# Residual additions of a feed-forward chunk placed between the next tile's taps, and squares summed later at its end

## The reference, cut to what matters

```
def conv_ffn(h, w_up, w_conv, b_conv, w_down):
    a = h @ w_up                                   # 1024 -> 5632
    a = conv1d(a, w_conv, width 3, causal, per channel) + b_conv
    g, val = split(a, 2)
    return (silu(g) * val) @ w_down                # 2816 -> 1024

x = x + conv_ffn(rms_norm(x, norm_ffn_g), w_up, w_conv, b_conv, w_down)
x = rms_norm(x, norm_final_g)                      # end of the first block
hx = modulate(rms_norm_2(x, norm_g), shift, scale) # start of the second block
p = hx @ a_w_in                                    # q, k, v and gate of the second block
```

## Time and profile before

| what | value |
|---|---|
| median of 3 runs | 3227.45 us (3226.65 to 3232.88) |
| the profiled execution | 3229.67 us, its span 3228.0 us, 44121 instructions |
| TensorE busy, matmuls | 2946.4 us, 91% |
| VectorE busy | 1726.4 us, 53% |
| GpSimd busy | 1067.0 us, 33% |
| ScalarE busy | 981.2 us, 30% |
| mean granted TensorE clock | 0.961 |

### The profile page before, as it was taken

How to read it: one execution, slowest core, us unless ns; L and a number is a source line. 1 busy time by engine, 2 the same in 40 slices (tenths; PEclk the granted TensorE clock), 3 DMA queues, 4 the chain that set the end, 5 groups by cost and what they waited for, 6 DMA issues and landing times. The chain is left out here.

```text
span 3228.0 us, 44121 instructions
## 1 busy us (share of the span) xinstructions
PE 2946.4 (91%) x16440; PEld 2420.9 (75%) x16440; DVE 1726.4 (53%) x2485; ACT 981.2 (30%) x1727; POOL 1067.0 (33%) x657
## 2 busy tenths in 40 slices
PE   3789899999999999989999997888889698999998
PEld 2578787777777777768877887878878477867776
DVE  4654254574455554555557337878752553067753
ACT  1112164321111111141101206767740200167731
POOL 1433312554554444432223221322233432311222
PEclk6899999999999999999999999999999899999999
DMA  2354460121111111113335312121111032342111
GB/s 85 126 171 157 126 137 21 33 72 39 45 47 57 46 39 44 40 39 114 126 129 182 131 60 106 51 98 50 58 35 39 24 123 93 111 119 53 28 40 66
DMA packets 214038, 255.18 MB, mean 79 GB/s; under 512 B 9385, under 2 KB 182766, under 8 KB 213886
## 3 DMA queue, kind: packets, MB, share of 16 engines
q1 hardware_dynamic: 198306, 189.68, 19.7%
q10 hardware_dynamic: 15584, 63.51, 5.0%
HBM read 187.56 MB, written 65.60 MB: 78 GB/s over the span
## 5 line engine op out<-in xcount | busy, mean ns | idle before, releaser
L977 PE MATMUL ps<-hh,w_parts 128*128 128x512 f32 (+2 forms) x2560 | 1000.7, 391 | 75.8 <-POOL hl L797 34.7
L978 PE MATMUL ps<-hl,w_parts 128*128 128x512 f32 (+2 forms) x2560 | 983.9, 384 | 0.0
L979 PE MATMUL ps<-hh,w_parts 128*128 128x512 f32 (+2 forms) x2560 | 981.3, 383 | 0.0
L977 PEld LDWEIGHTS ps<-hh,w_parts 128*128 128x128 f32 x2560 | 488.3, 191 | 193.2 <-issue 63.7
L758 POOL TENSOR_TENSOR w_parts<-w_raw,zero 128x1024 fp32r<-128x1024 f32 x140 | 289.5, 2068 | 975.3 <-PE ps L979 821.1
L978 PEld LDWEIGHTS ps<-hl,w_parts 128*128 128x128 f32 x2560 | 490.8, 192 | 104.5 <-issue 5.7
L979 PEld LDWEIGHTS ps<-hh,w_parts 128*128 128x128 f32 x2560 | 489.2, 191 | 99.8
L760 POOL TENSOR_TENSOR w_parts<-w_raw,w_parts 128x1024 fp32r<-128x1024 f32 x140 | 340.7, 2434 | 11.0
L1882 ACT ACTIVATE f_y<-f_z,convv 128x1024 f32<-128x1024 f32 x44 | 54.8, 1245 | 527.4 <-DVE f_z L2440 527.3
L977 PE MATMUL ps<-f_hi,d_hi 128*128 128x512 f32 x352 | 139.7, 397 | 19.8 <-DVE res L2477 13.8
L2616 DVE TENSOR_SCALAR_CACHE_REDUCE b_s<-ps 128x640 f32<-128x640 f32 (+1 forms) x128 | 100.0, 781 | 96.1 <-PE ps L1523 96.1
(11 more groups left out here) (338 smaller groups left out, 4866.6 us busy)
## 6 DMA issues: line engine op xcount, KB each, us to landing
w_mod_sb<-in_w_mod SPq DMA_DIRECT2D x16, 1536.0 KB, 7.0
w_raw<-in_w_up SPq DMA_DIRECT2D x44, 512.0 KB, 3.7
w_raw<-in_a_w_in SPq DMA_DIRECT2D x32, 512.0 KB, 4.0
d_raw<-in_w_down SPq DMA_DIRECT2D x22, 512.0 KB, 4.6
w_raw<-in_w_in SPq DMA_DIRECT2D x20, 512.0 KB, 5.0
za_parts<-z_hi ACTq DMA_DIRECT2D x16, 640.0 KB, 3.0
za_parts<-z_lo ACTq DMA_DIRECT2D x16, 640.0 KB, 4.1
d_even<-za_parts SPq DMA_DIRECT2D x16, 640.0 KB, 6.7
```

Of the source, the lines that this page charges most:

```text
L977: pe.matmul(out_, w_hi, x_hi, start=start, stop=False)
L978: pe.matmul(out_, w_hi, x_lo, start=False, stop=False)
L979: return pe.matmul(out_, w_lo, x_hi, start=False, stop=stop)
```

## The change

`ffn_taps` takes the number of the chunk whose additions it is to place (`adds`). In the loop the addition of row tile 0 goes between tap one and tap two of the value tile (s = 1), the addition of row tile 1 behind tap two, ahead of the product of gate and value. Row tiles 2 to 7 follow behind the product, where all eight stood. In the last chunk VectorE's order is new: the additions come with the low parts of the odd row tiles, the square of row tile m - 2 is summed behind addition m for m = 2 to 5, and the squares of row tiles 4 to 7 behind all additions. ScalarE squares row tiles 6 and 7 after the gain and the rounding of both.

```diff
-            def ffn_taps(chunk, e, acc_use, between=None):
+            def ffn_taps(chunk, e, acc_use, between=None, adds=None):
...
                     dve.scalar_tensor_tensor(f_y[:, s, 1:], f_z[:, 0:SEQ - 1], convv[:, bass.ds(tile + 2 * FT, 1)],
                                              f_y[:, s, 1:], ALU.mult, ALU.add).then_inc(f_tapped[s], 1)
+                    if s == 1 and adds is not None:
+                        add_down(adds, 0)
                     dve.wait_ge(f_tapped[s], 4 * chunk + (2 * e + 1))
                     dve.scalar_tensor_tensor(f_y[:, s, 2:], f_z[:, 0:SEQ - 2], convv[:, bass.ds(tile, 1)],
                                              f_y[:, s, 2:], ALU.mult, ALU.add).then_inc(f_tapped[s], 1)
+                if adds is not None:
+                    add_down(adds, 1)
                 dve.wait_ge(f_gate, 2 * chunk + (e + 1))
...
-            def ffn_down(chunk, norm=None):
+            def add_down(chunk, m):
+                if m < KT - 1:
+                    dve.wait_ge(f_down, 7 * chunk + (m + 1))
+                else:
+                    dve.wait_ge(d_used, chunk + 1 + 1)
+                dve.tensor_tensor(res[:, m, X_COLS], down_acc(m)[:, 0:SEQ], res[:, m, X_COLS], ALU.add).then_inc(acc_free[m % 2], 1)
+
+            def last_down(chunk, norm):
+
+                def add_square(k):
+                    norm_add(dve, norm, X_COLS, k // 2, k % 2, h_sum, h_sq[:, k % 2])
+
                 for m in range(KT):
...
+                    add_down(chunk, m)
+                    if m == 0:
                         norm_start(dve, norm, X_COLS, h_sum)
...
+                    if m and m % 2 == 0:
+                        low_part(dve, norm, m - 1, h_g[:, 1])
+                    if 2 <= m < 6:
+                        add_square(m - 2)
+                add_square(4)
+                add_square(5)
+                low_part(dve, norm, KT - 1, h_g[:, 1])
+                add_square(6)
+                add_square(7)
...
             with dve.Fori(1, CHUNKS) as c:
-                ffn_taps(c, 0, 6 * c - 4)
-                ffn_down(c - 1)
+                ffn_taps(c, 0, 6 * c - 4, adds=c - 1)
+                for m in range(2, KT):
+                    add_down(c - 1, m)
                 ffn_high(c, 0)
...
# ScalarE, last chunk
                 high_part(act, "a", k, h_g[:, s])
-                act.wait_ge(n_added[s], ADDED["a"] + k // 2 + 1)
-                act.activation(h_sq[:, s], res[:, k, X_COLS], ACT.Square, scale=a_weight[:, k:k + 1]).then_inc(n_squared[s], 1)
+                if k < 6:
+                    square_weighted(k)
+            square_weighted(6)
+            square_weighted(7)
```

More of the change, by code:

```diff
@@ L1899, in _, with square_weighted @@
             act.wait_ge(f_low, 2 * CHUNKS)
+            def square_weighted(k):
+                s = k % 2
+                act.wait_ge(n_added[s], ADDED["a"] + k // 2 + 1)
+                act.activation(h_sq[:, s], res[:, k, X_COLS], ACT.Square, scale=a_weight[:, k:k + 1]).then_inc(n_squared[s], 1)
             for k in range(KT):
@@ L2469, in context_parts @@
                 dve.tensor_tensor(hl[:, :, 0:CTX], c_g, hh[:, :, 0:CTX].bitcast(F32), ALU.subtract).then_inc(ctx_step, 1)
-            def ffn_down(chunk, norm=None):
-                for m in range(KT):
[L2473 to L2478, removed]
-                        norm_start(dve, norm, X_COLS, h_sum)
[L2480 to L2486, removed]
+            def add_down(chunk, m):
[7 more added lines that the diff above has]
+                    norm_add(dve, norm, X_COLS, k // 2, k % 2, h_sum, h_sq[:, k % 2])
+                for m in range(KT):
+                    add_down(chunk, m)
+                    if m == 0:
+                        norm_start(dve, norm, X_COLS, h_sum)
+                    if m and m % 2 == 0:
[7 more added lines that the diff above has]
+                add_square(7)
             ffn_taps(0, 0, 0)
@@ L2499, in _ @@
                 ffn_high(c, 1)
-            ffn_down(CHUNKS - 1, "a")
+            last_down(CHUNKS - 1, "a")
             norm_diagonals(dve, "a", SEQ, h_sq[:, 0])
```

## The result

The changed kernel took 3213.08 us (median of 5 runs, 3206.60 to 3213.11), the kernel before 3226.65 us in the same comparison (5 runs, 3224.10 to 3232.88). The ratio is 0.9948 with an interval of 0.9935 to 0.9961, so the change saves 12.6 to 21.0 us of 3226.65. The 3210 us and the 17.8 us of the prediction lie inside. The profiled execution took 3206.6 us (span 3204.9).

What follows compares the result with a forecast made beforehand. TensorE was taken to bound the kernel, stopped mainly by VectorE's late residual additions. Loop 15.6 plus last chunk 2.2 gives 17.8 us, from 3229.67 to 3211.9 or from the median 3227.45 to 3209.7; forecast 3210 us, range 3204 to 3217.

Steps and rivals of the forecast that it cites:

- The stop in the loop: TensorE's wait at the down product's 37th matmul goes: 1.55 us a body, 15.6 us over ten bodies.
- Addition 0 in time with 1.2 us of room: In the loop, addition 0 between the taps ends 1.2 us before row tile 3 is due, after about 0.1 us wait.
- Addition 1 with 1.5 us of room: In the loop, addition 1 behind tap two ends 1.5 us before row tile 4 is due.
- Tap one stays at 2.63, tap two at 1.28: Loop's value tile on VectorE: moved operations keep their length in us, as GpSimd rests during the moved tap two.
- The stall goes nowhere: In the loop, no other wait replaces the removed stop; the next thing late would be addition 0, 1.2 us from it.
- the second rival: Saved time is waited away at the next up tile: 3217.5 or 3225 us; whole stop staying or waited away, 0.03.
- The first: Rival: addition 0 still late in the loop, half gain 3217.5, none 3225 us; part of stop stays 0.07.
- The last chunk: Addition 7 ends at 1407.6 instead of 1409.83 because two sums go behind it: 2.2 us gained.
- The laid-out order: VectorE's step times in the last chunk, 1.13 us a step, three steps meeting GpSimd, addition 7 ending at 1407.6.
- The third rival: Last chunk's sums and low parts meet GpSimd oftener: 1 us lost, 3213 us; no chance of its own given.
- Sums 4 to 7 are hidden: Last chunk: these sums and low part 7 end about 1415.6, 7.8 us before TensorE wants the total.
- The clock, the rival of the other side: Without its pause in the loop TensorE drops to the low clock; with 5 us a body 3235 us; chance 0.04.

Runs made afterwards that it cites:

- c1: Changed kernel with the last chunk's old order on VectorE and ScalarE, so only the loop's additions moved: 3211.81 us, ratio 0.9960 to the kernel before.
- c2: Changed kernel with the loop's additions back behind the whole tap step, only the last chunk reordered: 3223.84 us, ratio 1.0002 to the kernel before.
- c4: Changed kernel with addition 0 moved behind tap two, beside addition 1 and ahead of the product: body 66.69 us, single run 3207.35 us.
- c5: Changed kernel with addition 1 back behind the product, addition 0 still between the taps: body 66.43 us, single run 3200.38 us.
- c3: Changed kernel with all sums of squares behind all additions, ScalarE's squares of row tiles 2 to 7 later: 3199.05 us, ratio 0.9933 to the kernel before.
- c0_again: The changed kernel run once more, unedited: 3203.68 us, ratio 0.9939 to the kernel before.

## Why the prediction was right, point by point

- **The stop in the loop, 1.55 us a body, 15.6 in all.** Right: 15.96 by A. The body went from 68.02 to 66.43, that is 1.59; it is 0.04 us a body more than forecast. Those 0.04 lie in the ten starts behind the 38th matmul, which the sum left out: in the kernel before they came 0.02 to 0.06 us later in all than in the changed one. c1 gives the term alone, c2 its absence.
- **Addition 0 in time with 1.2 us of room.** Right: 1.29 us. Its wait for the row tile, put at about 0.1 us, is there with some 0.07, though no idle time is listed: its row overlaps that of tap one by 0.02 us (1050.18 and 1050.16), where other rows back to back overlap by 0.09 (1052.58 and 1052.49). It starts 0.43 us after the 24th matmul's start (here 1049.73) in every body, also in the last, where tap one takes 2.70 us. So the row tile and no longer the tap decides when it starts. c4 shows that the room is real and short: behind one more tap the loop loses 0.26 us a body.
- **Addition 1 with 1.5 us of room.** It ends at 1053.71; row tile 4 is due 12 matmuls after 1052.68, at 1055.41: 1.7 us. Right; c5 shows that it need not have been moved.
- **Tap one stays at 2.63, tap two at 1.28, the addition at 1.21 to 1.23.** Right, but for a shortest addition of 1.20. Over the span (ns minimum, median, maximum):

```profile
L2487 DVE TENSOR_TENSOR res<-ps,res x88: 1204/1224/1225, 718.0 to 1390.8; 128x1024 f32<-128x1024 f32 x88
...
L2454 DVE SCALAR_TENSOR_TENSOR f_y<-f_z,convv,f_y x44: 1277/1283/3315, 661.8 to 1358.8; 128x1022 f32<-128x1022 f32 x44
```

- **The stall goes nowhere.** Right: the window of a body is busy throughout, so nothing is waited away at the next up tile, the second rival. The first, addition 0 still late, is answered by the 37th matmul.
- **The last chunk, 2.2 us.** Right: 2.11 by B, and by the same 2.11 the time from addition 0's start to addition 7's end fell (26.55 to 24.44). The laid-out order came true step by step: counted from addition 0's start, every step ends within 0.2 us of its forecast. Three steps meet GpSimd, as forecast: low part 1, sum 1 and sum 3 (VectorE's timeline).

```profile
1367.61 1.22 DVE L2487 TENSOR_TENSOR res<-ps,res 128x1024 f32<-128x1024 f32 x1 [5.44 <-PE ps L979]
...
1374.67 2.02 DVE L2077 TENSOR_TENSOR hl<-h_g,hh 128x1024 fp32r<-128x1024 f32 x1 [2.28 <-ACT hh L1606]
...
1378.88 2.73 DVE L2057 TENSOR_TENSOR h_sum<-h_sum,h_sq 128x1024 f32<-128x1024 f32 x1
...
1386.07 2.58 DVE L2057 TENSOR_TENSOR h_sum<-h_sum,h_sq 128x1024 f32<-128x1024 f32 x1
...
1390.84 1.21 DVE L2487 TENSOR_TENSOR res<-ps,res 128x1024 f32<-128x1024 f32 x1
1391.98 4.54 DVE L2057 TENSOR_TENSOR h_sum<-h_sum,h_sq 128x1024 f32<-128x1024 f32 x2
...
1397.57 2.57 DVE L2057 TENSOR_TENSOR h_sum<-h_sum,h_sq 128x1024 f32<-128x1024 f32 x2
```

  Addition 7 ends at 1392.05, 24.4 us after addition 0's start (24.3 forecast). The third rival, a loss here, fell.
- **Sums 4 to 7 are hidden with 7.8 us of room.** Right: they end at 1400.14, and the column sums start at 1408.32 with no wait, 8.2 us later. c3 spends that room: with eight sums and two low parts behind addition 7 it is gone by 0.38 us.
- **The clock, the rival of the other side.** It fell: clock 1.00 over the whole loop, without any pause (columns as in the earlier trace rows).

```profile
712.50:1354.30 641.80, 641.80 (x2784) 523.22 (x2784) 327.52 (x232) 90.82 (x76) 306.67 (x133) 1.00 0.15 46
```

  The slow restart behind the long stop stayed, as forecast: TensorE took 16.16 us from there to the column sums, and 15.70 before (1425.64 - 1409.94); the 0.46 more are within the 1.2 allowed.
- **The sum.** 17.8 forecast, 18.07 in the stages. The measured median, 3213.08, lies 3 us above the forecast of 3210. That is inside the spread of the runs and no term of the sum: c0_again, the same code, has a median of 3203.68.

## What to carry to other kernels

When a busy engine stops at the same place in every body, write down when its next operand is due and when the helper engine can first be there; the instruction that frees a bank belongs at the earliest point at which its data are ready, even between two steps of other work. One instruction's length can decide: behind tap two the same addition was already late. And where the gain is half a per cent, compare stages between fixed events of the profile, since those that the change touches repeated to 0.04 us while the stages around them moved by 5.8 and 8.5.

## What the runs showed of the hardware

**A pause that the list of waits does not show.** In c4 TensorE lost 0.26 us a body and no idle time stands in its rows, because a matmul's row (0.39 us) is longer than the distance of two starts (0.23). For the same reason the stop listed as 1.28 us put the 37th matmul off by 1.44 us; with the late starts behind it that is 1.59 us of a body (68.02 - 66.43).

**The restart of TensorE differed with the stop ahead of it.** Windows from the first matmul of the projection to the column sums, after and in c3_sums_last:

```profile
1392.10:1408.30 16.20, 16.14 (x72) 13.57 (x73) 7.78 (x5) 5.77 (x6) 3.20 (x1) 0.86 0.43 131
```

```profile
1377.50:1392.00 14.50, 14.34 (x72) 11.98 (x72) 13.70 (x10) 12.15 (x11) 2.51 (x1) 1.00 0.45 143
```

Behind 6.33 us of idle time the granted clock is 0.86 over the stretch, a part of it at the lower level of 1.2 GHz (the first matmul takes 0.76 us); behind 1.36 us it is 1.00 (0.47 us), and TensorE is at the column sums 1.4 us sooner (14.72 us in c3, with 0.38 of waiting in it, against 16.16). But c3 gives this back at once. Behind its column sums (16 narrow matmuls that take 1.92 us, after 0.38 us of idle time) the clock falls to the lower level, where the changed kernel, whose sums took 1.84 us without a wait, keeps the higher one. Why it falls there is not shown. Windows of c3 and of after, and then the 25th matmul behind the column sums in each:

```profile
1394.60:1398.00 3.40, 3.40 (x11) 2.83 (x10) 1.55 (x3) 0.00 (x0) 0.00 (x0) 0.51 0.00 0
...
1410.60:1414.00 3.40, 3.40 (x19) 2.89 (x18) 1.53 (x3) 0.00 (x0) 0.00 (x0) 1.00 0.00 0
```

```profile
1400.58 0.28 PE L977 MATMUL ps<-hh,w_parts 128*128 128x258 f32 x1
...
1415.06 0.28 PE L977 MATMUL ps<-hh,w_parts 128*128 128x258 f32 x1
```

From the projection's first matmul to that one c3 takes 23.03 us and the changed kernel 22.90. So shortening the stop beyond what the change does returned about the idle time and nothing for the clock: B and the way to that matmul together are 6.0 us shorter than after (21.37 + 23.03 against 27.52 + 22.90), the listed idle time of the two last stops 5.7 (6.33 + 0.75 - 1.36).

**The spread between executions sits in particular stages.** The head varied by 8.5 us and C by 5.8 us between profiles of kernels that do the same there, but for some sums of squares at the start of C. Which transfer or wait in them varies was not traced, and stays open.
